# Three one-time weight buffers for the eighth expert, and other chains at both ends of the expert loop

## The reference, cut to what matters

```
first_block:  h = rmsnorm(x, norm1_g);  x = x + hybrid_mixer(h, ...)      # phase A
              h = rmsnorm(x, norm2_g);  x = x + moe_ffn(h, ...)           # end of A, phase B
              x = rmsnorm(x, normf_g)                                     # end of B
second_block: hn = rmsnorm_2(x, norm_mix_2); projections, forgetting attention,
              gated delta rule; x = x + (gated branches) @ w_out_2        # phases C and E
              hn = rmsnorm_2(x, norm_ffn_2); x = x + conv-gated FFN(hn)   # phase D
              return rmsnorm_2(x, norm_final_2)

moe_ffn: 32 experts, the 4 best per token; for each expert
   gate = xb @ w_gate[e] + b_gate[e];  up = xb @ w_up[e] + b_up[e]        # 1024 x 1024 each
   gate = min(gate, 7);  up = clip(up, -7, 7)
   y = (gate * sigmoid(1.702 * gate) * (up + 1)) @ w_down[e] + b_down[e]  # 1024 x 1024
   out[token] += weight * y
```

## Time and profile before

| | |
|---|---|
| median of 3 runs | 1682.63 us |
| the profiled execution | 1682.89 us, of which the span is 1681.2 us |
| TensorE (PE) busy | 1650.0 us, 98% of the span |
| VectorE, ScalarE, GpSimd busy | 593.4, 454.8, 289.0 us |
| read from HBM | 505 MB, 302 GB/s over the span |

### The profile page before, as it was taken

The page is one execution under the profiler, slowest core; times in us unless marked ns, Lnnn a source line. Parts: engine busy times, 40 slices in busy tenths (PEclk is TensorE's granted clock), DMA queues, the critical chain, the costliest instruction groups (busy, mean ns, idle before and its releaser), DMA issues. The chain is left out here.

```text
span 1681.2 us, 22703 instructions
## 1 busy us (share of the span) xinstructions
PE 1650.0 (98%) x9176; PEld 949.6 (56%) x9176; DVE 593.4 (35%) x1128; ACT 454.8 (27%) x669; POOL 289.0 (17%) x187
## 2 busy tenths in 40 slices
PE   9999999999999999999999999999999999999998
PEld 7653333333333333333333333688999999999996
DVE  4234121212121212112111211675375244458852
ACT  3111111111111111101111110565555554454443
POOL 1110000000000000000000000434433614445553
PEclk9999999999999999999999999999999999999999
DMA  9567899999999999999999999543124214555552
GB/s 350 191 239 287 334 429 427 427 427 428 427 429 428 428 428 427 429 428 428 428 428 429 427 428 428 192 150 139 64 101 151 101 45 157 201 163 185 168 199 101
DMA packets 92905, 507.45 MB, mean 302 GB/s; under 512 B 8987, under 2 KB 32584, under 8 KB 68264
## 3 DMA queue, kind: packets, MB, share of 16 engines
q1 hardware_dynamic: 92696, 506.00, 74.7%
q10 hardware_dynamic: 144, 0.52, 0.1%
HBM read 505.46 MB, written 1.05 MB: 301 GB/s over the span
## 5 line engine op out<-in xcount | busy, mean ns | idle before, releaser
L1368 PE MATMUL ps<-ring,x 128*64 128x512 f32 x1536 | 338.1, 594 | 8.2 <-DMA ring<-in_w_up 8.2
L184 POOL TENSOR_TENSOR low<-ring,high 128x1024 fp32r<-128x1024 f32 x81 | 202.8, 2505 | 310.8 <-ACT high L181 310.7
L1368 PEld LDWEIGHTS ps<-ring,x 128*64 128x64 f32 x1536 | 107.3, 137 | 236.1 <-issue 216.4
L1480 PE MATMUL ps<-hTh,high 128*128 128x256 f32 x800 | 229.1, 286 | 4.7 <-DVE low L184 2.9
L1482 PE MATMUL ps<-hTh,low 128*128 128x256 f32 x800 | 227.8, 285 | 0.0
L1481 PE MATMUL ps<-hTl,high 128*128 128x256 f32 x800 | 227.7, 285 | 0.0
L181 ACT CAST high<-ring 128x1024 fp32r<-128x1024 f32 x162 | 168.7, 1048 | 206.8 <-PE ps L1482 136.0
L1399 PE MATMUL ps<-ring,x 128*64 128x512 f32 x768 | 175.4, 598 | 0.0
L1818 POOL MEMSET X<- 128x1024 f32 x1 | 1.0, 956 | 979.8 <-POOLq L1157 979.8
L184 DVE TENSOR_TENSOR low<-ring,high 128x1024 fp32r<-128x1024 f32 x81 | 111.4, 1375 | 148.5 <-ACT high L181 148.5
L1480 PEld LDWEIGHTS ps<-hTh,high 128*128 128x128 f32 x800 | 155.0, 194 | 6.6 <-issue 6.6
(11 more groups left out here) (442 smaller groups left out, 2234.6 us busy)
## 6 DMA issues: line engine op xcount, KB each, us to landing
ring<-in_w_down SPq DMA_DIRECT2D x53, 2048.0 KB, 27.3
ring<-in_w_gate SPq DMA_DIRECT2D x48, 2048.0 KB, 25.6
ring<-in_w_up SPq DMA_DIRECT2D x48, 2048.0 KB, 26.5
ring<-in_w_in SPq DMA_DIRECT2D x23, 2048.0 KB, 8.2
extra<-in_w_gate SPq DMA_DIRECT2D x16, 2048.0 KB, 23.3
extra<-in_w_down SPq DMA_DIRECT2D x16, 2048.0 KB, 30.1
extra<-in_w_up SPq DMA_DIRECT2D x14, 2048.0 KB, 28.1
ring<-in_w_up SPq DMA_DIRECT2D x22, 1024.0 KB, 6.5
```

The source lines that it names most:

```text
L184: eng.tensor_tensor(lo, self.raw(u), hi.bitcast(F32), ALU.subtract).then_inc(self.sem(who + "_split"), 1)
L1368: last = pe.matmul(bank[h * CAP:(h + 1) * CAP, :], xg[:, c, kh, :], w[:, c, h * 512:(h + 1) * 512], start=False, stop=kh == 1 and c == 3)
L1480: pe.matmul(out, wh, xh, start=start, stop=False)
```

## The change

1. **Pieces.** There are three one-time places, and they hold the pieces 45, 46 and 47 (second half of up, and both halves of down, of the eighth expert). All three add to one semaphore. Piece 47 is loaded first of all pieces, into memory that phase A doesn't use; 46 and 45 take the turns that 9 and 8 had. The pieces from 8 on go into the rotation at once. Eight experts are written out instead of four (`PEEL`). The loads 0 and 1 of phase C's ring wait for the end of gate and the first half of up of the last expert (before: first half of gate, and end of gate).
2. **Start of the loop.** The pick matrix of expert 0 is made at the end of phase A on VectorE, ahead of the counting of passes, and TensorE's gather of expert 0 follows in phase A. Eight of the `keep_busy` matmuls in phase B go and one of the three in phase A. The bias products stand ahead of the wait for `xg`. VectorE's preparations are reordered.
3. **Norms of rows** ("n2", "nn", "fin"): mean and eps are applied to the first half's sum (`row_half`) as soon as it is there, and ScalarE's root adds the second half's sum itself. For "n2" the scaling is in two halves, and the transposes wait for each.
4. **End of the loop.** The statistics of "nm" are worked out in phase B: tile 0 by `bn_stats` on VectorE, tile 1 by a sum of squares on ScalarE; one root gives both, and "nf" takes its own root later in phase C. `keep_busy` is 10 instead of 5 at the end of B, and 1 instead of 13 at the start of C. The transposes go row tile by row tile.
5. **Attention logits** of phase C: for two heads at a time, first the products with `sel` and the mask (fp32r), then those of q and k (fp32). Before, each head had them in the order sel, q with k, mask.

```diff
-    SPARE = 2
+    SPARE = 3
...
+    PEEL = 2
+    LATE = 45
...
-        return first and self.SLOTS <= n < self.SLOTS + self.SPARE
+        return first and self.LATE <= n < self.LATE + self.SPARE
...
-        return n if first and n < self.SLOTS else (n - self.SPARE) % self.SLOTS
+        return n % self.SLOTS if first and n < self.LATE else (n - self.SPARE) % self.SLOTS
...
-            for n, use in ((0, ("qk", 3)), (1, ("v", 1)), (2, ("u", 1)), (3, ("o", 1)), (9, ("pool", 1)),
-                           (6, ("ym", 1)), (7, ("ym", 1)), (4, ("out", 0, 1)), (5, ("out", 1, 1)), (8, ("out", 1, 1))):
+            pieces.load(sp, A, Pieces.LATE + 2, (Pieces.LATE + 2) // 6, True)
+            for n, use in ((0, ("qk", 3)), (1, ("v", 1)), (2, ("u", 1)), (3, ("o", 1)), (Pieces.LATE + 1, ("pool", 1)),
+                           (6, ("ym", 1)), (7, ("ym", 1)), (4, ("out", 0, 1)), (5, ("out", 1, 1)), (Pieces.LATE, ("out", 1, 1))):
...
-            for n in range(Pieces.SLOTS + Pieces.SPARE, 32):
-                used = n - Pieces.SLOTS - (Pieces.SPARE if n < 2 * Pieces.SLOTS + Pieces.SPARE else 0)
-                freed(used, used // Pieces.PER)
-                pieces.load(sp, A, n, n // Pieces.PER, True)
-            with sp.Fori(1, last) as rnd:
+            for n in range(Pieces.SLOTS, Pieces.ROUND * Pieces.PER * Pieces.PEEL + Pieces.SLOTS):
+                if not pieces.is_spare(n, True):
+                    used = n - Pieces.SLOTS - (Pieces.SPARE if n > Pieces.LATE else 0)
+                    freed(used, used // Pieces.PER)
+                    pieces.load(sp, A, n, n // Pieces.PER, True)
+            with sp.Fori(Pieces.PEEL, last) as rnd:
...
     def row_root(self, act, tag, n, t):
-        act.activation(c, c, ACT.Sqrt).then_inc(self.sem("norm_root"), 1)
+        act.wait_ge(self.sem("norm_squares"), self.squares_by(tag)[t])
+        act.activation(c, r, ACT.Sqrt, bias=c, scale=1.0 / D).then_inc(self.sem("norm_root"), 1)
+    def row_half(self, v, tag, n, t, eps):
+        v.wait_ge(self.sem("norm_squares"), self.half_squares_by(tag)[t])
+        v.tensor_scalar(c, c, 1.0 / D, eps, ALU.mult, ALU.add).then_inc(self.sem("norm_mean"), 1)
...
             for t in range(NT):
                 for h in range(2):
-                    v.wait_ge(sem("experts_summed"), 2 * t + h + 1)
+                    if t == 0:
+                        v.wait_ge(sem("experts_summed"), h + 1)
+                    elif h == 0:
+                        v.wait_ge(sem("norm_squares"), k.squares_by("nm")[0])
                     c = slice(h * 512, (h + 1) * 512)
                     v.tensor_tensor(x[:, t, c], total(t, h), env["gain"][:, c], ALU.mult).then_inc(sem("gained"), 1)
+                v.wait_ge(sem("gained"), 2)
+                chain.mark(v.bn_stats(half_stats[:, t, :], x[:, 0, t * 512:(t + 1) * 512]))
...
-            keep_busy(pe, banks.ps[:, DN, :], ones, 5)
+            keep_busy(pe, banks.ps[:, DN, :], ones, 10)
...
-            keep_busy(pe, banks.claim(pe, ("nm", 0)), ones, 13)
-            k.transposes(pe, banks, "nm")
+            keep_busy(pe, banks.claim(pe, ("nm", 0)), ones, 1)
+            for t in range(NT):
+                k.row_transposes(pe, banks, "nm", t)
...
+                for pair in ((0, 1), (2, 3)):
+                    halves = {h: banks.claim(pe, ("lo", hg, h)).rearrange("p (t s) -> p t s", t=NT) for h in pair}
+                    for h in pair:
+                        for rows_of in (row_high, row_low):
+                            pe.matmul(halves[h], sel[:, HG * hg + h, :],
+                                      rows_of[:, NEGC, :].unsqueeze(1).to_broadcast([8, NT, S]),
+                                      start=rows_of is row_high, stop=False)
+                    for h in pair:
+                        for t in range(NT):
+                            pe.matmul(halves[h][:, t, t * P:(t + 1) * P], ident_r[:, :], negmask[:, :], start=False,
+                                      stop=False)
+                    for h in pair:
+                        for t in range(NT):
+                            last = pe.matmul(halves[h][:, t, 0:(t + 1) * P], fqk[:, 0, h, t * P:(t + 1) * P],
+                                             fqk[:, 1, h, 0:(t + 1) * P], start=False, stop=t == NT - 1)
+                        banks.filled(last, ("lo", hg, h))
```

More of the change, by code:

```diff
@@ L395, in row_scale @@
             xs, xd = xs.rearrange("q (k p c) -> q k p c", k=2, c=4), order(xd)
-        v.tensor_scalar(xd, xs, r, None, ALU.mult).then_inc(self.sem("norm_scaled"), 1)
+            for h in range(2):
+                v.tensor_scalar(xd[:, h], xs[:, h], r, None, ALU.mult).then_inc(self.sem("norm_scaled"), 1)
+        else:
+            v.tensor_scalar(xd, xs, r, None, ALU.mult).then_inc(self.sem("norm_scaled"), 1)
     def row_transposes(self, pe, banks, tag, t):
@@ L488, in landed @@
         if self.is_spare(n, first):
-            pe.wait_ge(self.arrival(n, first), 16)
+            pe.wait_ge(self.spare_loaded, 16 * self.SPARE)
         elif first:
-            pe.wait_ge(self.loaded[s], 16 * (self.before[s] + 1 + (0 if n < self.SLOTS else (n - self.SPARE) // self.SLOTS)))
+            pe.wait_ge(self.loaded[s], 16 * (self.before[s] + 1 + (n if n < self.LATE else n - self.SPARE) // self.SLOTS))
         else:
@@ L913, in _ @@
             banks.moved(v, "rk")
-            chain.mark(v.tensor_scalar(slot[:, :, :], slot[:, :, :], -1.0, None, ALU.add))
+            chain(v.tensor_scalar(slot[:, :, :], slot[:, :, :], -1.0, None, ALU.add))
+            for t in range(NT):
+                v.tensor_scalar(env["pick"][:, t, :], iota_cap[:, 0, :], slot[:, t, 0:1], None, ALU.is_equal)\
+                    .then_inc(sem("picks"), 1)
             chain(v.reduce_max(cm[:, 0:1], cnt[:, :], AX.X))
@@ L1094, in _, with gather_rows @@
             banks.moved(pe, "lgt")
-            keep_busy(pe, banks.ps[:, banks.at["lgt"][0], :], ones, 3)
+            keep_busy(pe, banks.ps[:, banks.at["lgt"][0], :], ones, 2)
+            pe.wait_ge(banks.free[ROWS_BANK], banks.uses[ROWS_BANK])
+            pe.wait_ge(sem("picks"), NT)
+            gather_rows(pe, banks.ps[:, ROWS_BANK, :], env["pick"], xn).then_inc(banks.full[ROWS_BANK], 1)
+ROWS_BANK = 1
+def gather_rows(pe, bank, pick, xn):
+    for t in range(NT):
+        for h in range(2):
+            last = pe.matmul(bank[h * CAP:(h + 1) * CAP, :], pick[:, t, :],
+                             xn[:, t, h * 512:(h + 1) * 512], start=t == 0, stop=t == NT - 1)
+    return last
 def phase_b(nc, A, sem, sb, ring, banks, env):
@@ L1107, in phase_b @@
     pass0 = sb("pass0", [P, S // CAP + 1])
[L1108 removed]
+    pick = env["pick"]
     gpickT = sb("gpickT", [P, NT, P])
@@ L1197, in _, with gathered @@
         def _(v):
-            for t in range(NT):
-                v.tensor_scalar(pick[:, t, :], iota_cap[:, 0, :], slot[:, t, 0:1], None, ALU.is_equal)\
-                    .then_inc(sem("picks"), 1)
             chain = Chain(v, sem("dveB"))
+            def gathered(i):
+                bank = bank_take(v, G_, i)
+                gains = env["g2"][:, :].rearrange("p (h c) -> p c h", h=2).unsqueeze(3).to_broadcast([P, 4, 2, CAP])
+                bank_free(v.tensor_tensor(xg[:, :, :, :], bank.rearrange("p (c h j) -> p c h j", c=4, h=2), gains,
+                                          ALU.mult), G_)
+            v.tensor_scalar(hot[:, 0, :], ones[0:96, 0:CAP], fold[0:96, 0:1], None, ALU.mult).then_inc(sem("hot"), 1)
+            v.memset(gpickT[:, :, :], 0.0).then_inc(sem("zeroed"), 1)
+            for p in range(S // CAP + 1):
+                v.memset(pass0[:, p:p + 1], -float(p * CAP)).then_inc(sem("pass0"), 1)
+            gathered(0)
+            v.memset(y[:, :], 0.0).then_inc(sem("zeroed"), 1)
             v.wait_ge(sem("top_gates"), 1)
@@ L1290, in _ @@
             rows_kept(0)
+            act.dma_start(env["gain"][:, :], A["normf_g"].unsqueeze(0).to_broadcast([P, D]))\
+                .then_inc(sem("normf_in"), 16)
+            steps = act.snap(passes_of(act) * NE)
             with act.Fori(0, steps) as i:
@@ L1317, in gather @@
                 bank = bank_claim(pe, ROWS, i)
-                for t in range(NT):
-                    for h in range(2):
-                        last = pe.matmul(bank[h * CAP:(h + 1) * CAP, :], pick[:, t, :],
-                                         xn[:, t, h * 512:(h + 1) * 512], start=t == 0, stop=t == NT - 1)
-                bank_full(last, ROWS)
+                bank_full(gather_rows(pe, bank, pick, xn), ROWS)
             def turned(i):
@@ L1405, in expert @@
                 bank_full(last, DOWN)
-            for r in range(Pieces.ROUND):
+            for r in range(Pieces.ROUND * Pieces.PEEL):
                 expert(r, r, None)
-            with pe.Fori(1, pe.snap(passes_of(pe) * (NE // Pieces.ROUND))) as rnd:
+            with pe.Fori(Pieces.PEEL, pe.snap(passes_of(pe) * (NE // Pieces.ROUND))) as rnd:
                 for r in range(Pieces.ROUND):
```

(1 more changed line is left out.)

142 lines of the change are left out of this document (67 added, 75 removed).

## The result

| | time, us | runs | profiled execution |
|---|---|---|---|
| before | 1681.87 median (1677.56 to 1682.63) | 4 | 1682.89, span 1681.2 |
| changed | 1666.91 median (1666.37 to 1669.03) | 4 | 1666.37, span 1664.5 |

The ratio is 0.9915, 95% interval 0.9902 to 0.9927. So the change makes the kernel 15 us faster (12.3 to 16.5 by the interval). The prediction was 1668.7 us. Between the two profiled executions lie 16.7 us of span, where −13.9 was predicted.

A forecast was written before the change was run, and what follows sets the result against it. TensorE (28.25 us per expert) was taken to follow the weight transfers (29.40) once its lead is used up. −4.8 − 7.9 − 0.5 − 0.8 + 0.1 = −13.9 gave 1668.7 us against the median, range 1663.5 to 1674.

The forecast's parts named there:

- Start, −4.8: Start of the expert loop: first weight product near 142.6 instead of 147.42, through earlier scaling, picks and gather; −4.8 us.
- Pieces, −7.9: Weight transfers in the expert loop: moved one-time places shorten the stop, waits shrink from 13.5 to 5.6 us; −7.9 us.
- The 2.4 us for a restart: Weight transfers: estimated cost of restarting them at 151.12, used to reckon when they end before the next stop.
- only the bytes count: Rival on the weight transfers: the hole only moves and costs what it did, gain 4.9 instead of 7.9; 1671.7 us, 13%.
- the transfers keep up to the end: Rival on the weight transfers: no wait is left, all 13.5 us go; 1663.1 us, 12%.
- The restart hangs on something else, so the start is lost: Rival on the loop: restart not set by TensorE's use of piece 48, loop's end without the 4.8; 1673.5 us, 4%.
- End of the loop, −0.5: From T (end of the last down product) into phase C: earlier start, mostly lost to a new GpSimd wait; −0.5 us.
- the cover that the prediction named: Phase C: TensorE, arriving 1 to 4.5 us later, need not pay 2.9 us of VectorE wait and 1.7 of slow clock again.
- GpSimd bounds the seam: Rival on loop end and phase C start: GpSimd's unchanged 9.7 us make it cost +2.7 to +4; 1672 to 1673, 12%.
- does not hang on unit 1: Phase C: VectorE's chain (gate rows, low parts) behind the old 2.9 us wait was claimed independent of unit 1.
- Logits, −0.8: Attention logits of phase C: 16 changes of product kind become 8, at 0.1 us each; −0.8 us.
- "nn" and "fin", +0.1: Row norms "nn" and "fin": nothing in "nn", between −0.35 and +0.3 in "fin"; +0.1 us.

The follow-up runs named there:

- the pieces alone: Kernel before with only the third one-time buffer, places at pieces 45 to 47, two written-out rounds and the new order of the last two releases: 1673.08 us, ratio 0.9957.
- the start undone: Changed kernel with picks and gather of the first rows back in the expert phase, row statistics kept as changed: 1671.36 us, ratio 0.9937 to the kernel before.
- the two runs on place and number: Changed kernel with two one-time buffers at pieces 46 and 47 (1668.59 us), and with three at pieces 8 to 10 (1676.60 us).
- all but the pieces: Changed kernel with two one-time buffers at pieces 8 and 9 and one written-out round, as before: 1676.18 us, ratio 0.9972 to the kernel before.
- two late: Changed kernel with two one-time buffers in place of three, for pieces 46 and 47: 1668.59 us, ratio 0.9925 to the kernel before.
- three early: Changed kernel with its three one-time buffers at pieces 8, 9 and 10: 1676.60 us, ratio 0.9975 to the kernel before.
- 69 to 71: Changed kernel with three written-out rounds and the three one-time buffers at pieces 69 to 71: 1663.48 us, ratio 0.9898 to the kernel before.
- the edits together: Changed kernel with one-time buffers at pieces 69 to 71, GpSimd's low part of unit 1 ahead of the masks, residual multiplications behind the third pair: 1660.16 us, ratio 0.9880.
- the buffers at 93 to 95: As the edits together, but with a fourth written-out round and the one-time buffers at pieces 93 to 95: 1659.96 us, ratio 0.9876 to the kernel before.

## Why the prediction was right, step by step

- **Start, −4.8: measured −4.9.** The gather starts at 137.66 and the first weight product at 142.50 (142.6 predicted). The run without the step loses 4.45 us between the medians and 4.17 in its first weight product; the other 0.75 is in the row statistics.
- **Pieces, −7.9: measured −8.9 in the profile, −8.2 as the pieces' own run.** The mechanism is the predicted one: a stop near 370, its end set by TensorE's use of piece 48, issue at 372.43 where 377.1 − 4.8 = 372.3 was reckoned. The term was 1.0 short because of one number: a restart and a landing cost 1033.36 − 372.43 − 134 × 4.90 = 4.3 us, not the 5.6 taken over from the stop of before. (The same sum gives 4.5 with the pieces alone and 4.6 with the start undone, but 5.2 with the stop at the old place and all else changed, over 172 pieces. Whether the restart was cheaper or the 4.90 is 0.01 too small over the longer way is not told apart.) The 2.4 us for a restart, which the prediction takes for the end of the transfers before the stop, does not follow from the window named for it, where 1.2 us at most are lost; it sets the length of the stop and not the time, which hangs on the use of piece 48. Four experts wait, not five, from 945 on, not 915. The two rivals on this step fell: "only the bytes count" by the two runs on place and number, "the transfers keep up to the end" by the four waits.
- **The restart hangs on something else, so the start is lost:** fell. With the start undone the restart comes 4.16 us later, and with the old pieces the start still brings its 5.
- **End of the loop, −0.5: measured −0.4** (13.84 at T, 14.21 at 1104.18). Its parts were less right. Phase C starts at T + 7.6 (7.9 predicted) and its first product at T + 12.6, where T + 11.4 was predicted: the scaling took 2.82 us instead of 1.62 beside GpSimd's memsets. The new wait is 2.8 (3.3), unit 1 comes at T + 18.6 (17.7). That the sum came out so near is in part luck, as these misses cancelled. The clock's price of 1.7 at the new wait was not paid in the profile of the changed kernel. Five of the six other profiles that have this wait have a drop right behind it, and in these the later wait for VectorE is 0.7 or less (or not listed) instead of 2.1: the cover that the prediction named. The sixth, all but the pieces, has no drop there and 2.1, as the changed kernel; but it has one behind the wait of 2.1, and `XT,ones` stands at T + 210.46 in it. With a drop at the new wait and no other on the way it is T + 208.49, 208.96 and 208.50 (two late, three early, 69 to 71), with none T + 208.96: a drop at the new wait costs nothing in the end, one behind VectorE's wait costs 1.5 us. In the run with 69 to 71:

```profile
1066.00:1068.00 2.00, 2.00 (x15) 2.00 (x14) 1.97 (x3) 0.00 (x0) 2.00 (x1) 0.72 0.00 0
1068.00:1070.00 2.00, 2.00 (x11) 2.00 (x11) 2.00 (x2) 0.00 (x0) 1.86 (x4) 0.50 0.08 7
```

- **The rival "GpSimd bounds the seam"** was wrong as a sum and right on the cause. GpSimd's unchanged order is what the seam lost its gain to: with its low part first the rows up to `XT,ones` are 3.4 us shorter, with the residual moved too 4.7 (2.2 and 3.0 between the medians). The prediction's sentence that VectorE's chain "does not hang on unit 1" is the one that failed: it hangs on GpSimd's subtractions for units 1 and 3 (1.2 us) and, as these decide who comes first, on the pair behind the masks (2.2 us).
- **Logits, −0.8: measured −1.0** in the profile with the waits behind (0.57 and 0.45 in the ledger), and −0.57 per group between the products.
- **"nn" and "fin", +0.1: measured 0.** Both last stretches take 6.7 us.
- **Not in the sum: −1.5.** A drop of the granted clock in the profiled execution of before, near 1280, that no edit removed. Without it the difference of the profiles would be 15.2, beside 15.0 between the medians and 13.9 predicted.

Between the predicted 1668.7 and the measured 1666.91 lie 1.8 us. Of these 0.8 are the kernel before: its fourth run brought its median from 1682.63 to 1681.87. The other 1.0 is the pieces' term. What stays open is why the profile of the changed kernel has no drop behind its new wait, while most others have.

## What to carry to other kernels

A one-time buffer ahead of a ring gives nothing while the transfers already wait for a free place: it only moves and lengthens the stop (waits of 14.0 us with three at the ring's start, 13.5 with two). Put it at the place in the stream where the consumer has caught up on the producer by as much as the buffers hold; from the rate of both (here 4.71 and 4.90 us per piece) that place can be reckoned (an estimate from these: 3 × 4.71 / 0.19, some 74 pieces; at 45 the transfers still stopped, at 69 they did not), and the window with the fallen GB/s shows whether it was met. Before counting a wait as cover for another, look which other engine's work lengthens the chain that ends it: a shift of one GpSimd instruction of 2.4 us brought the end of VectorE's chain from T + 51.36 to T + 47.96.

## What the runs showed of the hardware that I had not expected

A drop of TensorE's granted clock without a rest that the profile shows. The windows of before around 1278:

```profile
1276.00:1278.00 2.00, 2.00 (x9) 1.33 (x9) 1.32 (x6) 1.98 (x5) 0.05 (x1) 1.00 0.38 62
1278.00:1280.00 2.00, 2.00 (x14) 2.00 (x14) 0.99 (x5) 1.99 (x3) 0.00 (x0) 0.77 1.00 373
1280.00:1282.00 2.00, 2.00 (x12) 2.00 (x11) 2.00 (x4) 2.00 (x6) 0.00 (x0) 0.50 1.05 410
```

TensorE is busy in all of each window, and the grant is at half, the level of 1.2 GHz, for some 3 us. Ahead of it, from 1272.38, ran eight products with `ones` and eight with 8 rows. The changed kernel runs the same instructions at 1.00; of the twelve profiles of the experiments seven have a drop at this place. Each costs 1.4 to 1.5 us: from `XT,ones` to the last product it is 398.5 us in the six profiles without it and 400.0 in those with it (400.4 with the old order of the logits). The drop near 48 us looks alike: from 43.66 to 45.9 TensorE of before runs products with 4 rows, without a rest that the profile shows, and from 46 to 50 the grant is 0.72 and 0.50. No run changed these products, so the cause stays open. The Trainium skill, "TensorE: Matmul & The Clock Gate", Part 1, ties the halved clock to an engine that has been idle; these windows show it without a rest, and here the measurement decides. Drops go together with much of the spread of one kernel's runs: with the edits together the run of 1657.71 us has a mean grant of 0.999 and the three of 1659.96 to 1660.54 have 0.997; with the buffers at 93 to 95 the grants 0.999, 0.998, 0.997 and 0.996 go with 1657.50, 1659.18, 1660.74 and 1662.04 us.
